# Mixing layer of a decoder step: part-array runs split, keys rotated ahead of the mLSTM outputs, head factors and three copies on ScalarE

## What is computed

```
def head_norm(h, g, center):
    if center:
        h = h - h.mean(-1, keepdims=True)
    var = jnp.square(h).mean(-1, keepdims=True)
    return (h * lax.rsqrt(var + HEAD_EPS)).reshape(B, T, H * dh) * g

def retention_group(qc, kc, vc, gc, s0, g, pos0):
    q = rotary(qc.reshape(B, T, H_C, DK_C), pos0)
    k = rotary(kc.reshape(B, T, H_C, DK_C), pos0) * DK_C ** -0.5
    ...
    y, _, s1, _ = chunk_scalar_decay(q, k, v, log_f, log_i, s0, ...)
    out = jax.nn.silu(gc) * head_norm(y, g, True)

def mixing_block(x, st, l, P, lb, pos0):
    proj = jnp.einsum('btd,de->bte', x, P['w_in'][l])
    (xa, ga, qb, kb, vb, ob, ib, fb, qc, kc, vc, gc, qd, fd, id_, gd) = jnp.split(proj, cuts, axis=-1)
    ya, h1, buf1 = rglru_group(...)
    yb, c1, n1, m1 = mlstm_group(...)
    yc, sr1 = retention_group(...)
    yd, sh1 = hgrn2_group(...)
    mixed = jnp.concatenate([ya, yb, yc, yd], axis=-1)
    out = jnp.einsum('bte,ed->btd', mixed, P['w_out'][l])
```

## Time and profile before

| | us |
|---|---|
| median of 3 runs | 1003.19 |
| lowest, highest | 997.62, 1004.17 |
| profiled execution, its own time | 1000.41 |
| its span in the trace | 998.6 |
| mean granted clock of PE | 0.994 |

### The profile page before, as it was taken

The page is one execution under the profiler, slowest core; times in us unless marked ns, Lnnn a source line. Parts: engine busy times, 40 slices in busy tenths (PEclk is TensorE's granted clock), DMA queues, the critical chain, the costliest instruction groups (busy, mean ns, idle before and its releaser), DMA issues.

```text
span 998.6 us, 23743 instructions
## 1 busy us (share of the span) xinstructions
PE 975.8 (98%) x10672; PEld 809.6 (81%) x10672; DVE 502.5 (50%) x1032; ACT 187.2 (19%) x410; POOL 80.6 (8%) x105
## 2 busy tenths in 40 slices
PE   9999999999999999999999999999999999999995
PEld 6897887999999999998988879567776867778643
DVE  6898884764666654268978875330101201011135
ACT  1433232221111000044332332300000000000001
POOL 1101032500000000000000200230000020000020
PEclk9999999999999999999999999999999999999998
DMA  9437248224443155201233488899999999999982
GB/s 358 148 108 256 85 169 358 85 82 173 169 173 128 70 193 220 111 26 60 89 126 108 147 320 325 332 326 387 402 420 400 422 390 414 422 424 423 421 323 80
DMA packets 37499, 241.43 MB, mean 242 GB/s; under 512 B 5009, under 2 KB 8145, under 8 KB 17681
## 3 DMA queue, kind: packets, MB, share of 16 engines
q1 hardware_dynamic: 27280, 216.69, 55.0%
q0 software_dynamic: 6432, 19.43, 5.6%
q10 hardware_dynamic: 3680, 3.74, 1.3%
HBM read 228.60 MB, written 13.07 MB: 242 GB/s over the span
## 4 chain that ended last, share of the span: by engine, by line
PE 87%; DVE 11%; issue 1%; ACT 0%; DVEq 0%
PE ps L773 65%; PE ps L1401 15%; PE ps L1509 6%; PE ps L776 1%; DVE small L2482 1%; PE ps L1338 1%; DVE overlay L2260 0%; DVE overlay L2259 0%; DVE up_slots L2629 0%; DVE overlay L2653 0%; DVE overlay L2445 0%; DVE overlay L2487 0%; DVE up_slots L2632 0%; DVE mix_or_moe L2443 0%; ACT x L1858 0%
## 5 line engine op out<-in xcount | busy, mean ns | idle before, releaser
L773 PE MATMUL ps<-up_slots,mix_or_moe 128*32 128x352 f32 (+2 forms) x3248 | 240.6, 451 | 2.7 <-DVE overlay L2774 1.9
L773 PEld LDWEIGHTS ps<-up_slots,mix_or_moe 128*32 128x32 f32 (+2 forms) x3248 | 150.4, 111 | 83.5 <-issue 10.4
L773 PE MATMUL ps<-x,up_slots 128*128 128x144 f32 (+3 forms) x832 | 151.3, 337 | 0.0
L773 PEld LDWEIGHTS ps<-x,up_slots 128*128 128x128 f32 x832 | 126.0, 191 | 23.1 <-issue 6.1
L773 PE MATMUL ps<-overlay,tables 128*32 128x256 f32 (+4 forms) x1992 | 123.4, 375 | 1.2 <-DVE overlay L2260 1.0
L773 PEld LDWEIGHTS ps<-overlay,tables 128*32 128x32 f32 (+2 forms) x1992 | 100.9, 113 | 19.6 <-DVE mix_or_moe L2778 2.0
L3159 DVE TENSOR_TENSOR mix_or_moe<-mix_or_moe,ps 128x352 f32<-128x352 f32 x24 | 11.3, 518 | 173.7 <-PE ps L773 173.7
L1401 PE MATMUL ps<-overlay,up_slots 128*128 128x144 f32 x704 | 91.7, 286 | 0.6 <-DVE overlay L2935 0.3
L1401 PEld LDWEIGHTS ps<-overlay,up_slots 128*128 128x128 f32 x704 | 88.4, 190 | 1.1 <-issue 0.8
L773 PE MATMUL ps<-up_slots 128*128 128x144 f32 (+2 forms) x768 | 84.1, 280 | 0.0
L773 PEld LDWEIGHTS ps<-up_slots 128*128 128x128 f32 (+2 forms) x768 | 79.0, 186 | 2.3 <-issue 0.8
(11 more groups left out here) (379 smaller groups left out, 998.4 us busy)
## 6 DMA issues: line engine op xcount, KB each, us to landing
up_slots<-in_moe_w SPq DMA_DIRECT2D x64, 1408.0 KB, 23.1
overlay<-in_moe_w SPq DMA_DIRECT2D x21, 1536.0 KB, 25.5
up_slots<-in_ffn_w SPq DMA_DIRECT2D x30, 1024.0 KB, 6.9
up_slots<-in_w_in SPq DMA_DIRECT2D x27, 1024.0 KB, 4.9
up_slots<-in_w_out SPq DMA_DIRECT2D x8, 1024.0 KB, 7.3
overlay<-in_moe_w SPq DMA_DIRECT2D x7, 1024.0 KB, 25.3
mix_or_moe<-in_states POOLq DMA_DIRECT2D x6, 512.0 KB, 5.0
expert_tokens<-in_shape_tables POOLq DMA_DIRECT2D x8, 384.0 KB, 6.5
```

The lines of the kernel that those rows point to most:

```text
L773: return pe.matmul(o, lhsT, rhs, start=start, stop=stop)
```

## The change

It does five things, in both layers.

1. On PE the last two products of panel 3 move from ahead of the mLSTM outputs to a place between `sample_outputs` and `carried`, and two products of panel 4 move from behind the retention scores to ahead of `value_rows` of HGRN2.
2. On DVE the rotation of the keys moves from behind `merge_sample()` to ahead of `mlstm_outputs()`. ACT issues the four DMAs of the key's swap earlier (after the mLSTM values); those of the queries stay. The swapped keys go to another place in scratch.
3. On DVE `merge(5, 2)` moves ahead of `keys(6, 0, "ml_dv")`.
4. The three head factors are made on ACT alone as exp(-0.5 ln(var + eps)): Ln, a wait for its own semaphore `rstd_ln`, Exp. The three reciprocals leave DVE.
5. The three copies (HGRN2 keys, `Y_HG`, `Y_RET`) go from DVE to ACT.

```
-        rotmp = cut(MB, 6924, 2, T), cut(MB, 6924 + 576, 2, T)
+        rotmp = cut(scr, 7866, 2, T), cut(MB, 6924 + 576, 2, T)
@@ PE, mix(l)
                 lru_gates()
-                seven(3, 3, 7)
+                seven(3, 3, 5)
                 need("lru_ac", "tanh")
...
                 sample_outputs(B_, value(0), sample_weight)
+                seven(3, 5, 7)
                 carried(B_, state(0), QH[:, 0])
...
                 head_mean(C_, Y_ML, "ml_ps")
-                seven(4, 2, 3)
+                seven(4, 2, 5)
...
                 end(scores(C_, QC, KC, 1), "ret_ps", "s23")
-                seven(4, 3, 7)
+                seven(4, 5, 7)
@@ ACT, mix(l)
+                def half_swap(i, tile_at, landed):
+                    act.wait_ge(*ev(tile_at + 1, l))
+                    for block in range(0, P, HD // 2):
+                        other = block ^ HD // 2
+                        act.dma_start(rotmp[i][block:block + HD // 2], proj[other:other + HD // 2, tile_at:tile_at + 2]
+                                      ).then_inc(landed, 16)
...
-                def head_dev(bank, sd, name):
+                def head_rstd(rr, sd, src, floor, name):
+                    f(sd, src, ACT.Ln, bias=floor).then_inc(S["rstd_ln"], 1)
+                    rstd_count[0] += 1
+                    act.wait_ge(S["rstd_ln"], rstd_count[0])
+                    end(f(rr, sd, ACT.Exp, scale=-0.5), name, "rr")
+
+                def head_dev(bank, rr, sd, name):
                     need(name.replace("_ac", "_ps"), "var")
-                    end(f(sd, PS[:, bank, 0:T], ACT.Sqrt, bias=HEAD_EPS), name, "sd")
+                    head_rstd(rr, sd, PS[:, bank, 0:T], HEAD_EPS, name)
...
                 values(4, 0, "ml_ac")
+                half_swap(0, KC, S["swap_k_in"])
                 seven(3, 0)
...
                 seven(4, 2)
+                need("hg_ps", "keys")
+                f(KTK[:, 0, 0:2, :], PS[:, 4, :].rearrange("p (t c) -> p t c", t=2), ACT.Copy)
+                end(f(SAMPLE_KEYS[0], PS[:, 5, 0:HD], ACT.Copy), "hg_ac", "keys")
                 seven(5, 0)
                 need("ml_dv", "vs")
-                end(f(SD_ML, SD_ML, ACT.Sqrt, bias=VAR_FLOOR), "ml_ac", "sd")
+                head_rstd(RR_ML, SD_ML, SD_ML, VAR_FLOOR, "ml_ac")
...
                 seven(6, 0)
+                need("hg_ps", "out")
+                end(f(Y_HG, PS[:, 4:6, 0:T], ACT.Copy), "hg_ac", "y")
...
                 seven(6, 1)
+                need("ret_ps", "out")
+                end(f(Y_RET, PS[:, 2:4, 0:T], ACT.Copy), "ret_ac", "y")
                 seven(6, 2)
@@ DVE, mix(l)
+                merge(5, 2)
                 keys(6, 0, "ml_dv")
-                merge(5, 2)
...
                 lru_gain()
+                rotate(0, KC, "rot_k")
                 mlstm_outputs()
...
                 merge_sample()
-                rotate(0, KC, "rot_k")
                 rotate(1, QC, "rot_q")
```

More of the change, by code:

```diff
@@ L110 @@
     "hg_dv": "kneg kb q x0 x1 l0 x2 l1 m0 x3 l2 m1 l3 m2 m3 x4 x5 l4 m4 l5 x6 m5 ends l6 m6 m7 hk m7s "
-             "keys c0 c1 y states rr n",
-    "hg_ac": "kexp qtanh ln z0 z1 z2 z3 z4 z5 z6 ends vt sq sd",
+             "c0 c1 states n",
+    "hg_ac": "kexp qtanh ln z0 z1 z2 z3 z4 z5 z6 ends vt keys y sq rr",
     "ret_ps": "s01 s23 keys vt pstate out states mean var rb",
-    "ret_dv": "rot_k rot_q qs w01 w23 keys y pstate states ctr rr n",
-    "ret_ac": "vt sq sd",
+    "ret_dv": "rot_k rot_q qs w01 w23 keys pstate states ctr n",
+    "ret_ac": "vt y sq rr",
     "ml_ps": "ma01 ma23 s01 s23 vt keys out pstate states mean var rb",
-    "ml_dv": "qs w01 w23 keys y pstate states ctr vs rr n",
-    "ml_ac": "e01 e23 vt y sq sd",
+    "ml_dv": "qs w01 w23 keys y pstate states ctr vs n",
+    "ml_ac": "e01 e23 vt y sq rr",
     "th_ac": "ga2 ga GD GC OB",
@@ L1252, in mix @@
                 value_rows(A_, VC, (0, 1))
-                need("hg_dv", "keys")
+                need("hg_ac", "keys")
                 for c in range(2):
@@ L1270, in mix @@
                         mm(o[h][:, P:SEQ], value(2)(1, 2 * p + h), AT[:, 1, 2 * p + h], True, False)
-                need("ml_dv", "rr")
+                need("ml_ac", "rr")
                 head_scale(C_, RR_ML, "ml_ps")
@@ L1294, in mix @@
                 seven(6, 5, 7)
-                need("ret_dv", "y")
+                need("ret_ac", "y")
                 sample_states(A_, 1, VM_RET, 3, "ret_ps")
@@ L2010, in mix @@
                 end(f(om_[:, :, 0:WC], om_[:, :, 0:WC], ACT.Sqrt, scale=-1.0), "lru_ac", "sqrt")
-                for i, (tile_at, landed) in enumerate(((KC, S["swap_k_in"]), (QC, S["swap_q_in"]))):
-                    act.wait_ge(*ev(tile_at + 1, l))
-                    for block in range(0, P, HD // 2):
-                        other = block ^ HD // 2
-                        act.dma_start(rotmp[i][block:block + HD // 2], proj[other:other + HD // 2, tile_at:tile_at + 2]
-                                      ).then_inc(landed, 16)
+                half_swap(1, QC, S["swap_q_in"])
                 tile(16)
@@ L2035, in mix @@
                 need("ml_dv", "states")
-                need("hg_dv", "y")
+                need("hg_ac", "y")
                 end(f(SQ_HG, Y_HG, ACT.Square), "hg_ac", "sq")
@@ L2478, in center @@
                     end(tt(y, y, PS[:, bank:bank + 2, 0:T], SU), name, "ctr")
-                def head_rstd(rr, sd, name):
-                    need(name.replace("_dv", "_ac"), "sd")
-                    end(v.reciprocal(rr, sd), name, "rr")
                 def head_scale(bank, y, g, name):
@@ L2747, in mix @@
                 panel_sums(5)
-                need("hg_ps", "keys")
-                cp(KTK[:, 0, 0:2, :], PS[:, 4, :].rearrange("p (t c) -> p t c", t=2))
-                end(cp(SAMPLE_KEYS[0], PS[:, 5, 0:HD]), "hg_dv", "keys")
                 keys(2, 1, "ret_dv")
@@ L2772, in mix @@
                 panel_sums(7)
-                need("ret_ps", "out")
-                end(cp(Y_RET, PS[:, 2:4, 0:T]), "ret_dv", "y")
                 need("hg_ps", "states")
```

21 lines of the change are left out of this document (9 added, 12 removed).

## The result

The changed kernel takes 991.15 us (median of 20 runs, 986.37 to 997.11), the kernel before 1001.45 us (median of 20 taken with them, 994.99 to 1005.85). The ratio is 0.9907, with a 95% interval from 0.9888 to 0.9926: 0.9% faster, by 7 to 11 us. I had forecast 996.0 us, 7.2 us of gain counted from the 1003.2 us then known, with a range of 990 to 1001. Against the 1001.45 us measured beside it the gain is 10.3 us by the medians, 9.6 us by the means (991.42 us of 20 runs, against 1000.99 us of the 75 runs of the kernel before that were taken beside the experiments; the 20 beside it have 1000.80), and 11.7 us between the two profiled executions (988.68 and 1000.41 us).

A forecast was written before the change was run, and what follows sets the result against it. PE, busy 975.8 of 998.6 us, was taken as the bound. Waits of 0.9 + 2.5 + 1.9 + 0.3 = 5.6 us plus 1.65 us of clock, less 0.1, gave 7.2 us off 1003.19: 996.0 us, range 990 to 1001.

The forecast's parts named there:

- both waits go: 2.5 us: Mixing, both layers: moving the key rotation removes PE's waits for the query rotation and the centring, 1.27 us a layer.
- PE also gets two products more to do ahead of that place (part 5): Before the query rotation and centring: two moved products give PE extra work there; no gain of their own was counted.
- I count no gain there: Panel output PE transposes next: key copy frees DVE, PE loses about 2 us of cover; 0.15 us more wait a layer allowed.
- What is late next: After `Y_RET`: DVE's addition of the HGRN2 sample states comes next, with 0.3 to 0.6 us of slack remaining.
- I expect the clock not to fall there: First piece of tile 16, layer 1: with the part-array run cut, 4.83 us becomes 3.18, gaining 1.65 us; bounds 0 to 6.6.
- moving two products costs no time by itself: PE in mixing: the eight matmuls moved keep their durations, so the move itself costs 0 us.
- (b): Timed runs had more clock falls than the profiled one and the splits remove them: 12.1 us gained, 991.1 us; chance 0.19.
- (a): Clock falls as before or at another uncut part-array run; only the waits go, 5.5 us, 997.7 us; chance 0.22.
- (c): Head factors on ACT: each function switch costs twice what the rows show, 5.0 us of 7.2 lost, 1001.3 us; chance 0.05.
- (d): Layer 0: DVE waits for the keys' swap; each us beyond 88.4 costs one, landing at 97.6 gives 1005.2 us; chance 0.03.
- (e): Experts: weights don't come earlier, so layer 1's gain is lost, 2.3 + 1.65 us less, 999.9 us; chance 0.05.

The follow-up runs named there:

- second trace of before: Profile of the kernel before, run once more without any edit as an experiment: 999.31 us (12 runs), ratio 0.9986.
- splits alone: Kernel before with only the product moves on PE (two of panel 3 later, two of panel 4 earlier): 994.68 us, ratio 0.9961.
- rotation alone: Kernel before with only the key rotation moved ahead of the mLSTM outputs and its swap issued earlier: 993.94 us, ratio 0.9952.
- copies alone: Kernel before with only the three copies (HGRN2 keys, `Y_HG`, `Y_RET`) moved to ACT: 995.36 us, ratio 0.9962.
- factors alone: Kernel before with only the three head factors made as Ln and Exp on ACT: 997.82 us, ratio 0.9976.
- the long run: Kernel before with 40 more part-array matmuls ahead of the mLSTM outputs in each layer: 1019.94 us (6 runs), ratio 1.0169.
- one split: Changed kernel with panel 4's products put back as before and POOL's weight sums in halves: 989.08 us (6 runs), ratio 0.9894.

## Why the prediction came out, point by point

PE's lead over the second trace of before, in us, by place (falls of the clock and PE's own issue left out; both layers together unless said):

| place | whole change | splits alone | rotation alone | copies alone | factors alone | forecast |
|---|---|---|---|---|---|---|
| merge, layer 0 | 0.8 | 0 | 0 | 0 | 0 | 0.9 |
| query rotation and centring | 3.4 | 3.4 | 3.4 | 0 | 0 | 2.5 |
| panel output behind them | 0.3 | -1.1 | 0 | 0.9 | 0 | -0.1 |
| `Y_RET` | 2.4 | 0 | 0 | 2.4 | 0 | 1.9 |
| retention factor | 0.5 | 0 | 0 | 0 | 0.5 | 0.3 |
| LayerNorm, layer 0 | 1.0 | 0 | -0.1 | 1.1 | -0.1 | none |
| broken runs | -0.4 | -0.4 | 0 | 0 | 0 | 0 |
| PE's lead in all | 8.0 | 1.8 | 3.2 | 4.4 | 0.4 | 5.5 |

The timed runs agree. Without the clock's share the mean of the changed kernel is 7.9 us below that of before (985.7 against 993.6); the splits alone 2.3, the rotation alone 3.9, the copies alone 4.2, the factors alone 1.2, each with an error of 0.5 to 0.7. The clock's share is 5.7 us (error 0.3) where the 75 runs of before have 7.4. The two together are the 9.6 us. The 8.0 us of waits are shown; that the 1.7 us belong to the change is not, as told below.

- **Part 1, the merge.** 0.8 us against 0.9, with 0.2 left of the wait, in layer 0 alone. Right.
- **Part 2, the keys rotated early.** The mechanism was right, and the swap had landed. Two things were off. The size: recorded waits of 0.61 and 0.67 us were worth 1.68 a layer, so "both waits go: 2.5 us" was 3.4. And the step "PE also gets two products more to do ahead of that place (part 5)" was only a remark, where it needed a test: by itself it removes the same waits. The term belongs to part 2 or to part 5, and is earned once; singly the parts sum to 10.6 us with the merge, together they give 8.0.
- **Part 3, the copies.** The step "I count no gain there" at the panel output was too cautious (0.9 us alone; in the whole change the lost cover of the split eats most of it, 0.3 is left). `Y_RET` gave 2.4, not 1.9. "What is late next" was nothing. The 1.0 us at LayerNorm is the term that I had none for, and it was luck: it comes of where DVE's sums begin against POOL's instructions, and the long run got 0.8 us of that wait off without any edit there.
- **Part 4, the factors.** 0.5 us against 0.3, at the place named.
- **Part 5, the splits.** "I expect the clock not to fall there" held in the profile: 4.83 us became 3.18, the 1.65 us forecast, and the mean share of the clock is lower by 1.7 us. But the reason isn't shown to be the split. The kernel before itself takes 3.18 us at this piece of layer 1 in its second trace and falls in layer 0 instead, so the two profiled executions alone show nothing; that forecast and share agree in size is luck as far as the runs tell. The step "moving two products costs no time by itself" failed: the first split costs PE 0.2 us a layer, 0.4 in all. The second costs nothing itself, but takes 0.26 us a layer of cover from the panel output, and has no use where the rotation is moved.

**The clock, as far as it could be settled.** In the eight traces of kernels whose run ahead of tile 16 isn't cut (without the long one) a fall stood at tile 16 in 6 of 16 layers; in the five traces with the cut, in none of 10. If the cut had no part in it and all 26 layers were alike, drawing all 6 falls from the 16 has a chance of 8008/230230, about 3 in 100. The mean share of the clock in the timed runs is 5.4 us (50 runs, error 0.2) with the cut and 5.9 (66 runs, error 0.2) in the edited kernels without it. So the cut may be worth about 0.6 us, just under twice the error of the difference (0.3). The kernel before has 7.4 in its 75 runs but 6.2 (12 runs, error 0.5) in those taken as an experiment, so over 1 us of the 1.7 may be a difference between sets of runs and none of the change's. What part of the 1.7 is the change's stays open. A long run of part-array products isn't enough for a fall, as the run of 13.8 us shows, and a short one has had it.

My rival (b) gave 991.1 us, the time that was measured, but from falls at two places in both layers of the timed runs. The clock's share fell by no more than 1.7 us. The 991 came about by larger terms for the waits, so (b) was right by number and wrong by mechanism.

**The other rivals.** (a), the clock falls anyway at tile 16: not in any trace with the cut. (c), a table switch costs twice: no drain in the rows, and no wait for the factor; the Trainium skill ("ScalarE: Activation LUTs", section "What ACT_TABLE_LOAD costs") gives 1380 ns of draining besides the load, and the rows at 148.67 and 149.97 us leave room for none. (d), DVE waits for the swap: no idle time ahead of 86.31 us. (e), the weights of the experts hold PE: the changed kernel's lead over the second trace of before passes through the steady part of the experts unchanged, within 0.01 us from 680 to 960 us.

**What moves an execution by 6 us.** Between traces the lead changes most at the start of the experts. There PE waits for the tokens of expert 1, and DVE, which turns them, for the landing of their transfers (it stands idle for 11 to 13 us in the five traces looked at), which POOL issues while the experts' weights come in (DMA share 0.96 to 1.06 in the windows from 636 to 660 us of four traces). The wait was, by trace: 0 (first of before, one split), 0.6, 1.1, 1.3, 1.4, 1.4 and 1.8 us, all without a fall behind them; 2.1, 2.2, 2.3, 3.8 and 4.8 us, all with one (at 4.8 it began 0.5 us before the wait ended); and 2.7 us without. A fall costs 1.7 us. So an execution with a late landing loses up to 5.5 us at this one place (about 6.3 with the long run), in kernels of either order. The wait is the larger part of it; that it also causes the fall behind it is argued from the order of the two, and the one wait of 2.7 us without a fall speaks against a fixed rule. The profiled executions differ by 11.7 us, where the means differ by 9.6, for another reason: the first of before also had a fall at tile 16, 1.7 us, and its own 1.6 us at 970 us. The Trainium skill ("TensorE: Matmul & The Clock Gate", section "Why this matters for your kernels") wants no long idle gaps of PE between bursts. A fall at five of the six gaps over 2 us agrees with it, and so does the lower level over the idle end of all traces; the falls at tile 16, with no gap ahead, don't.

## What to carry to other kernels

- Cost two edits that cover the same wait together, not one after the other: what either gives alone tells nothing of the second. Here the leanest set (merge, rotation, copies, with POOL's sums in halves) has the whole gain in waits, 8.8 us of lead against 8.0 of the full change.
- Work taken off an engine pays only up to the next place where that engine waits for the bottleneck; look for that place in its timeline (the 1.95 us of the reciprocal vanished in an idle time of 2.36 us that became 4.12).
- When effects of 1 us are sought in executions that scatter by 6, lay traces side by side by the starts of the same instruction and read the steps; and split the timed means into the clock's share and the rest. Run the unchanged kernel as an experiment too: here its clock's share alone moved by over 1 us.

## What the hardware showed that I had not expected

- DVE's sums of x (tensor-tensor, both operands in SBUF) that run beside a sum of POOL end 0.2 to 0.4 us behind the start of POOL's next instruction. A sum of 128x288 took 2.5 us beside POOL instructions of 2.35 to 2.6 us and 1.41 us beside ones of 1.3 to 1.5 us, and 0.69 to 1.06 us where it began 0.3 to 0.7 us ahead of such a boundary. Halving POOL's instructions brings PE 1.3 us. The Trainium skill ("SBUF — State Buffer", section "SBUF: two separate sides") says that the two engines share one pair of ports under an exclusive lock, held for a whole instruction, also where a DVE instruction has two SBUF inputs and POOL's reads SBUF; the rows agree: the wait goes by the length of POOL's instruction, and not by bytes. I had not applied it at a place where the prediction saw no edit.
- A wait of PE that goes entirely is worth more than its recorded idle time: 0.94 (with 0.11 at the instruction behind it) gave 1.18, 0.16 gave 0.23, 0.61 and 0.67 gave 1.68, 0.94 at the last sum of x gave 1.1 to 1.3. A wait that only changes counts at its own size: the merge's went from 0.99 to 0.18 us and gave 0.81, the panel output's grew from 0.24 to 0.80 and cost 0.56. No run tested why.
- A fall of the clock inside the span lasted 3.4 us and cost PE, where it was busy, 1.7 us, every time (tile 16 took 4.87 us for 3.18), and the same instructions had it in one execution of a kernel and not in the next.
